# A two-network trunk in fp32 on one core: modulation chunks in the first steps of the first network's mixer, and the second network's output squares on ScalarE

## What is computed

```python
def modulation(cvec, w_mod, b_mod):
    m = (jax.nn.silu(cvec) @ w_mod + b_mod)[..., None, :]
    return jnp.split(m, 6, axis=-1)
...
    # first network, a layer
    u = (rmsnorm(x, g_mix) * (1 + sc1) + sh1) @ w_in
    mix = jnp.concatenate([pool_mixer(...), gla_output(...), latent_attention(...)], axis=-1) @ w_out
    x = x + ga1 * mix
    x = x + ga2 * squared_relu_mlp(rmsnorm(x, g_mlp) * (1 + sc2) + sh2, w_up, w_down)
...
    # second network, a layer
    h = rmsnorm_2(x, g_mix_pre[l]) * (1.0 + scale_a) + shift_a
    y = hybrid_mixer(h, ...)
    x = x + gate_a * rmsnorm_2(y, g_mix_post[l])
    h = rmsnorm_2(x, g_ffn_pre[l]) * (1.0 + scale_f) + shift_f
    x = x + gate_f * rmsnorm_2(swiglu(h, w_gate_up[l], w_down[l]), g_ffn_post[l])
```

## Time and profile before

| | us |
|---|---|
| median of 3 runs | 1969.89 (1969.11 to 1974.73) |
| the profiled execution | 1973.71 |
| its span, first to last instruction | 1971.9 |
| TensorE busy (matmul) | 1767.2 (90%) |
| VectorE busy | 1117.6 (57%) |
| ScalarE busy | 688.5 (35%) |
| transfers | 309 MB, mean 157 GB/s |

### The profile page before, as it was taken

How to read it: one execution, slowest core, us unless ns; L and a number is a source line. 1 busy time by engine, 2 the same in 40 slices (tenths; PEclk the granted TensorE clock), 3 DMA queues, 4 the chain that set the end, 5 groups by cost and what they waited for, 6 DMA issues and landing times.

```text
span 1971.9 us, 25716 instructions
## 1 busy us (share of the span) xinstructions
PE 1767.2 (90%) x10636; PEld 1419.1 (72%) x10636; DVE 1117.6 (57%) x1768; ACT 688.5 (35%) x832; POOL 84.6 (4%) x87
## 2 busy tenths in 40 slices
PE   5997996999999998989689996997899979779997
PEld 2785553777777777764269995776799756659996
DVE  2664764464444445746267675565766565566654
ACT  2413334141213223433243443353333233633331
POOL 0020000010000001100000000000100010010000
PEclk7998797999999999978789998998899989889999
DMA  8321395123344433325754555531455563325552
GB/s 331 126 89 43 133 357 216 64 86 128 135 158 138 156 140 141 103 90 207 276 180 171 192 197 184 197 128 44 150 174 188 177 209 130 129 93 185 172 177 80
DMA packets 172372, 309.21 MB, mean 157 GB/s; under 512 B 3264, under 2 KB 54720, under 8 KB 171616
## 3 DMA queue, kind: packets, MB, share of 16 engines
q1 hardware_dynamic: 168592, 293.98, 42.7%
q10 hardware_dynamic: 3376, 12.02, 1.7%
q0 software_dynamic: 288, 1.57, 0.2%
HBM read 305.46 MB, written 2.10 MB: 156 GB/s over the span
## 4 chain that ended last, share of the span: by engine, by line
PE 75%; DVE 13%; ACT 5%; DMA 4%; issue 1%; POOL 1%; DVEq 0%; SPq 0%; ACTq 0%
PE bank L556 57%; PE twin L556 15%; DVE ring_r L1195 4%; PE bank L565 3%; ACT arena_r L1937 3%; DMA ring<-in_w_in 2%; ACT arena L1937 1%; DVE arena L1195 1%; DMA ring<-in_w_mod 1%; DMA ring<-in_w_out 1%; POOL rs L2324 1%; DVE params L1195 1%; DVE arena L1279 1%; DVE arena_r L1195 1%; DVE X L1689 1%
## 5 line engine op out<-in xcount | busy, mean ns | idle before, releaser
L556 PE MATMUL bank<-arena_r 128*128 128x512 f32 (+2 forms) x2128 | 703.1, 377 | 15.7 <-DVE arena_r L1807 6.7
L1195 DVE TENSOR_TENSOR ring_r<-ring,arena_r 128x4096 fp32r<-128x4096 f32 (+4 forms) x94 | 393.6, 4188 | 250.3 <-ACT arena_r L1937 249.5
L1937 ACT ACTIVATE arena_r<-ring 128x4096 fp32r<-128x4096 f32 (+4 forms) x94 | 323.1, 3437 | 441.5 <-PE bank L556 157.4
L556 PEld LDWEIGHTS bank<-arena_r 128*128 128x128 f32 x2128 | 406.4, 191 | 96.0 <-issue 7.7
L556 PE MATMUL twin<-actT_r,arena_r 128*128 128x256 f32 x1408 | 255.3, 284 | 0.4 <-DVE actT_r L1195 0.4
L556 PE MATMUL bank<-ring_r,arena_r 128*128 128x512 f32 x624 | 245.8, 394 | 0.0
L556 PE MATMUL bank<-arena_r,actT_r 128*128 128x512 f32 (+3 forms) x624 | 217.0, 379 | 9.9 <-issue 3.6
L556 PEld LDWEIGHTS twin<-actT_r,arena_r 128*128 128x128 f32 x1408 | 220.7, 193 | 0.9 <-DVE actT_r L1195 0.8
L1937 ACT ACTIVATE arena<-bank 128x512 f32<-128x512 f32 (+6 forms) x183 | 87.4, 477 | 359.7 <-PE bank L556 292.4
L556 PE MATMUL twin<-actT_r,ring_r 128*128 128x256 f32 x704 | 199.6, 284 | 0.0
L556 PE MATMUL bank<-ring_r,actT_r 128*128 128x512 f32 (+3 forms) x496 | 182.5, 368 | 0.0
(11 more groups left out here) (193 smaller groups left out, 1753.7 us busy)
## 6 DMA issues: line engine op xcount, KB each, us to landing
ring<-in_w_mod SPq DMA_DIRECT2D x24, 2048.0 KB, 9.3
ring<-in_w_ada SPq DMA_DIRECT2D x24, 2048.0 KB, 8.7
ring<-in_w_gate_up SPq DMA_DIRECT2D x44, 1024.0 KB, 7.7
ring<-in_w_down SPq DMA_DIRECT2D x20, 2048.0 KB, 7.8
ring<-in_w_up SPq DMA_DIRECT2D x16, 2048.0 KB, 7.8
ring<-in_w_in SPq DMA_DIRECT2D x12, 2048.0 KB, 8.8
ring<-in_w_out SPq DMA_DIRECT2D x8, 2048.0 KB, 12.4
ring<-in_w_down SPq DMA_DIRECT2D x8, 1792.0 KB, 7.6
```

What stands on the lines that cost most here:

```text
L556: ins = nc.tensor.matmul(out_, lhsT, rhs, start=start, stop=stop)
L1195: return v.tensor_tensor(o, x, y, op)
L1937: return nc.scalar.activation(o, x, func, **kw)
```

## The change

In the first network's mixer, layer 0 does its sixteen chunks in steps 0 to 15 and not 6 to 21, and copies the sums in step 18 and not 22. Layer 1 does its twelve in steps 0 to 7 and 9 to 12 and not 3 to 14, and copies the sums (of the batch that ends with the eighth chunk) in step 8 and not 11. The order of the loads is the same.

In the second network the squares of y go to ScalarE, which reads the bank (`squares2`) and sums each half into columns of `ss` of its own. VectorE waits for them (`gsq_ready`), makes the mean, and multiplies the bank by the gate into `y2`, without the copy. The bank is free after that. `mark["y", ...]` only records in TensorE's program how many banks were filled.

```diff
-WEIGHTED1, FILLS1, SUMS1 = [[2, 6, 10, 14], [2, 6]], [range(6, 22), range(3, 15)], [22, 11]
+WEIGHTED1, FILLS1, SUMS1 = [[2, 6, 10, 14], [2, 6]], [range(0, 16), (0, 1, 2, 3, 4, 5, 6, 7, 9, 10, 11, 12)], [18, 8]
...
                     for t in range(TS):
                         b = filled()
-                        y = y2[:, t, c]
-                        step(v.tensor_copy(y, b[:, :]), v_emptied)
-                        squares(junk2, y, t)
                         mean = ms[:, t:t + 1]
+                        dve.wait_ge(gsq_ready, nth(gsq_ready))
                         if half == 0:
                             step(v.tensor_scalar(mean, ss[:, t:t + 1], 1.0 / D, EPS, ALU.mult, ALU.add))
-                            step(tt(y, y, GA[:, 0, c], ALU.mult))
                         else:
 
-                            v.scalar_tensor_tensor(out=mean, in0=ss[:, t:t + 1], scalar=1.0 / D, in1=mean,
+                            v.scalar_tensor_tensor(out=mean, in0=ss[:, 2 + t:3 + t], scalar=1.0 / D, in1=mean,
                                                    op0=ALU.mult, op1=ALU.add).then_inc(ms_ready, 1)
                             handed.append(("power", t, 1))
-                            step(tt(y, y, GA[:, 0, c], ALU.mult))
+                        step(tt(y2[:, t, c], b[:, :], GA[:, 0, c], ALU.mult), v_emptied)
...
+            def squares2(l, stage, half):
+
+                n = mark["y", l, 2 * stage + half] - TS
+                for t in range(TS):
+                    act.wait_ge(v_filled, n + t + 1)
+                    step(f(junk2, VB[(n + t) % 2][:, :], ACT.Square, accum_out=ss[:, 2 * half + t:2 * half + t + 1]),
+                         gsq_ready)
...
                 split(after(("out2", l, 0)))
                 high_latents(1, filled())
+                squares2(l, 0, 0)
                 split(after(("out2", l, 1)))
+                squares2(l, 0, 1)
...
                 for c in range(2 * len(HC2)):
                     split(after(("down2", l, c)))
+                    if c % 3 == 2:
+                        squares2(l, 1, c // 3)
```

More of the change, by code:

```diff
@@ L1116, in layer2 @@
                 banks = [take("v") for t in range(TS)]
+                mark["y", l, 0] = k["v"]
                 for i in range(KT):
@@ L1132, in layer2 @@
                     linear(b[:, :], mixed(t), lambda i: [x[:, i, :] for x in w], filled)
+                mark["y", l, 1] = k["v"]
                 normed([0, 1], 2 * (L + l) + 1)
@@ L1143, in layer2 @@
                     banks = [take("v") for t in range(TS)]
+                    mark["y", l, 2 + half] = k["v"]
                     for c, (k0, k1) in enumerate(HC2):
```

## The result

| | before | after |
|---|---|---|
| median, us | 1969.5 (1967.51 to 1974.73, 4 runs) | 1952.01 (1949.87 to 1955.53, 4 runs) |
| profiled execution, us | 1973.71 | 1949.87 |
| its span, us | 1971.9 | 1948.1 |
| TensorE busy, us | 1767.2 | 1763.6 |
| VectorE busy, us | 1117.6 | 1095.9 |

The ratio after to before is 0.9909 with an interval of [0.9884, 0.9933]: faster, by 17.5 us of medians where 32.2 were forecast. 1952.0 lies above the range (1930 to 1949). Two repeats of the changed kernel gave 0.9910 [0.9897, 0.9923] and 0.9893 [0.9875, 0.9910]. The two first profiles are 23.8 us apart because that of before is one of its slower executions and that of after its fastest; a pair taken later, 1971.5 and 1953.5, is 18.0 apart.

A forecast was written before the change was run, and what follows sets the result against it. TensorE was taken to bound the kernel, holding 75% of the chain, so only its waits could shrink. Terms 11.3 + 11.9 + 9.0 = 32.2 us took the 1969.9 us median to 1937.7, range 1930 to 1949.

The forecast's parts named there:

- Layer 0's mixer, 11.3 us: First network, layer 0: chunks moved to steps 0 to 15 let ScalarE's split of out1 begin earlier; 11.3 us gained.
- what would show it: Listed signs: layer 0's split waits for no load, TensorE's 12.28 us wait falls under 3, step 3's scores wait 1.6.
- Layer 1's mixer, 11.9 us: First network, layer 1: out1's load goes out earlier, so ScalarE's split begins at 960.5, not 972.49; 11.9 us gained.
- the two ends that were given: Layer 1's mixer: gain 11.9 us with out1 there at 960.5, or 6.5 if its load took 13.3 us from issue.
- Squares, 9.0 us: Second network, after out2 and down2: squares on ScalarE and no copy on VectorE shorten handovers and tails; 9.0 us.
- The ends: Tails after the last matmuls: 2.85 us gained at down2's end in layer 0, 0.65 at the kernel's end.
- The squares lie under VectorE's 4.44 us split: Between down2's halves: squares hidden by VectorE's split, so TensorE starts 1.25 us earlier, twice, 2.5 in all.
- The prediction's own sign of being wrong: VectorE's rows waiting for ScalarE's squares for more than 1 us outside the last tile.
- TensorE's own matmuls do not change here, so a gain can only come from time in which TensorE waits: Whole kernel: TensorE's matmul time taken as unchanged, so only its waits at the mixers and second network's projections were counted.
- All rivals on the clock: First network's mixers: half clock at the end (0.14), clock kept at the start (0.11), whole mixer slower (0.03).
- The first rival: Layer 0's mixer, steps 16 to 20: without chunks TensorE falls to 0.68 clock, 7.5 us more, 1945; chance 0.14.
- The second rival: Layer 0's mixer, stretch 200 to 220: clock rises from 0.68 to 1.00, 6.4 us less, 1931; chance 0.11.

The follow-up runs named there:

- the last experiment: Layer 0's last two chunks in steps 20 and 21, sums copied in step 22, against the kernel with three later edits together: 1942.87 us, 0.9849.

## Why the prediction was wrong

**Layer 0's mixer, 11.3 us: the mechanism came, the number in part by luck.** The two pairs, and the first kernel before with the changed kernel of the second repeat, gave 11.8, 9.5 and 10.3. The split, the waits and step 3's scores came as listed under what would show it. But the granted clock from 199 to 302 is 0.87 before and 0.90 after, an estimated 3 us of the 11.8 (103 us by 0.03) for which the sum had nothing. Against it, TensorE waits 1.78 us for ScalarE at 301.50, which the sum had not either. And low stretches that come and go move this stretch: 3.6 us in the run of the squares alone, with the old mixer.

**Layer 1's mixer, 11.9 us: mis-sized.** At the split it was 9.4 us (22.35 less the 12.95 with which the layer began), and 8.1 by the end of the mixer in both pairs, as the last wait there is 2.03 us and was 0.73. The step that failed took a load of 7.7 us, the minimum of the earlier trace rows, for the one ahead and 5.4 us for the one behind; it was 9.4 and 6.7. Out1's own load was thus put at 7.8 us from issue to landing and took 11.4; in the kernel before it took 11.7, and the median of the chunks' loads was 9.1. The wait left at the split, forecast as 6 us, is 8.96. The truth lay between the two ends that were given, 6.5 and 11.9, and the favourable end was taken.

**Squares, 9.0 us: some 7.** Alone they gave 7.1 us with an interval that holds 9.0, so it is the rows that show what was missing. The ends held: behind down2 of layer 0, 2.8 us came where 2.85 were forecast, and the time from the kernel's last matmul to X went from 2.36 to 1.69 us:

```profile
1938.93 0.39 PE L556 MATMUL bank<-arena_r 128*128 128x512 f32 x1
...
1939.42 0.60 ACT L1937 ACTIVATE params<-bank 128x512 f32<-128x512 f32 x1 [4.07 <-PE bank L556]
...
1940.24 0.16 DVE L1683 SCALAR_TENSOR_TENSOR ms<-ss,ms 128x1 f32<-128x1 f32 x1 [4.00 <-ACT params L1937]
...
1941.03 2.61 DVE L1689 SCALAR_TENSOR_TENSOR X<-params,rs,X 128x1024 f32<-128x1024 f32 x2
```

A square is 0.60 us, and 0.82 with the read of its sum until VectorE goes on; 0.78 was taken. The step that failed is "The squares lie under VectorE's 4.44 us split" for down2's first half: it had read VectorE's rows at the handover, but not TensorE's, whose last matmul into the second bank stood at 1553.38, behind the end of the split at 1552.77:

```profile
1553.38 0.39 PE L556 MATMUL bank<-arena_r 128*128 128x512 f32 x1
...
1555.95 0.47 PE L556 MATMUL bank<-arena_r 128*128 128x512 f32 x1 [2.19 <-DVE params L1675]
```

TensorE's wait there went from 2.19 to 1.90 us: twice 0.3 us in place of twice 1.25. The prediction's own sign of being wrong, VectorE waiting over 1 us for a square outside the last tile, came with 1.02 us at this place.

**The clock: the miss that counts.** The step that failed is the prediction's premise "TensorE's own matmuls do not change here, so a gain can only come from time in which TensorE waits". They did change, by the clock: the same matmuls took 9.3 us longer in four stretches. The mechanism's terms together give some 25 us in the second pair (9.5, 8.1, some 7 for the squares, 0.7 of the first loads); 7 of these went, net, with what later stretches gave back, at out1 of layer 1, the two in2 and the half clock at down2's second half. Of the 14.2 us missing in that pair (32.2 less 18.0) the clock is thus about half, layer 1's mixer 3.8, layer 0's 1.8 and the squares 2. All rivals on the clock looked at the mixers' own steps, where the chunks move. None asked what a shift by some 10 us does to work that starts after a wait, hundreds of microseconds on. The first rival (half clock in steps 16 to 20) did not come: 287 to 302 ran at 1.00, 287 to 307 at 0.91. Its mechanism is real, though, as the last experiment shows at 0.60; there the chunks of steps 14 and 15 are gone from ahead of these steps. The second rival (the start keeps its clock) came in part: 200 to 220, 0.68 before, is 0.86 in the same steps:

```profile
199.00:219.00 20.00, 18.59 (x216) 11.74 (x219) 14.71 (x36) 7.35 (x14) 0.00 (x0) 0.86 0.79 284
```

The prediction set the Trainium skill, TensorE: Matmul & The Clock Gate, section "Part 1: The HAM clock gate", against the trace: throttled by default, released by activity. The same section says that the chip's observation runs on freely and doesn't start with the kernel's work; that was the sentence to weigh, for by it a shift alone can change the clock. The runs here agree: equal waits of 17.6 and 17.45 us, followed by 3 or by 9 us at half clock. What stays open is the half clock in down2's second half of layer 0 (3.4 us at half clock, the stretch 1.6 us longer), present in two of three profiles of the changed kernel and not tried by itself; and what it is in the end of layer 1's mixer that takes the clock from out1.

## What to carry to other kernels

In this kernel, where TensorE worked again after a wait of 10 to 20 us, its first 3 or its first 8 to 9 us ran at half clock, and which of the two it was depended on when the work began; so an edit anywhere ahead gave or took 2 to 3 us at each such place. Count these places before forecasting a gain, and fill the wait with matmuls, real ones that can be moved there or, failing that, idle ones; here both, with one bank freed earlier, gave 7.8 us. A premise that other work keeps its time has to be checked in the granted clock of that work, before and after. An operation is hidden under another engine's work only if its input is ready by then, which is to be read from the rows of the engine that makes the input.

## What the runs showed of the hardware

- Ahead of in2, with waits of 10.6 to 19.6 us, the clock fell 2.7 to 4.3 us after TensorE's last matmul, and rose 2.8 to 4.3 us or 7.9 to 9.5 us after work began again, never in between, in the 22 places of eleven profiles (both layers, no idle matmuls). A delay of TensorE by about 2 us moved the rise from the second group to the first, in both layers.
- A busy TensorE lost the clock too: 18.00 of 18 us busy at a granted clock of 0.60, with narrow matmuls.
- 18 idle matmuls of 128x128 by 512, 15.72 us together, right behind real work kept the clock at full through a wait of 17 us.
- A load of 2 MB issued 4.7 us behind another took 11.1 to 12.2 us to land, where a load with none ahead of it and 0.5 MB of GpSimd's beside it took 9.4.
